# A hybrid decoder step with an expert lookup: tile border, sample path and depthwise convolution rearranged

## The reference, cut to what matters

```
x += W_out [ window attention | conv branch ] (rmsnorm(x) W_in)
x += peer(rmsnorm(x))
x += (p W_ple) * sigmoid(rmsnorm(x) W_gate)

conv branch: y[t, c] = sum over j < 31 of w[j, c] * glu[t - 30 + j, c] + bias[c]; layer norm; silu   (512 channels)
peer:        for each token 8 heads x 16 experts = 128 choices (top 16 of each of two key lists per head, then top 16 of their 256 sums)
             act = gelu(u[choice] . h); x += sum over the 128 choices of softmax weight * act * v[choice]
```

## Time and profile before

| | |
|---|---|
| time, median of 3 (range) | 3282.76 us (3281.87 to 3284.22) |
| profiled execution: its own time, its span | 3279.73 us, 3278.0 us |
| mean granted TensorE clock | 0.92 |
| busy share: TensorE, VectorE, ScalarE, GpSimd | 79%, 78%, 38%, 30% |
| mixer (until the first gather) | about 579 us |
| experts | about 2699 us |
| gathers | 1032, 1082 MB |

### The profile page before, as it was taken

One profiled execution on the slowest core, in us unless ns is written; L12 is line 12 of the kernel. 1 busy time (PEld: TensorE's weight loads), 2 busy tenths in 40 slices (PEclk: granted clock), 3 DMA queues, 4 the chain that ended last, 5 costly groups with the idle time before them and its releaser, 6 DMA issues.

```text
span 3278.0 us, 28593 instructions
## 1 busy us (share of the span) xinstructions
PE 2598.7 (79%) x8010; PEld 1279.4 (39%) x8010; DVE 2543.9 (78%) x5806; ACT 1252.6 (38%) x3574; POOL 999.5 (30%) x1072
## 2 busy tenths in 40 slices
PE   6899898777877788778777877787778777878778
PEld 3555444433433343334333433343334333434322
DVE  4889884898886888688868886888688868885555
ACT  2332323343443334433443344334433443344233
POOL 1000000343433333333333333333333333333241
PEclk8999998899999898999989988998989889989899
DMA  6000003999999999999999999999999999999996
GB/s 208 20 26 32 26 29 123 415 406 420 420 408 420 420 420 399 420 420 416 403 420 420 416 400 420 420 419 400 419 420 419 396 420 420 420 404 418 403 397 268
DMA packets 169961, 1144.79 MB, mean 349 GB/s; under 512 B 21376, under 2 KB 25072, under 8 KB 36688
## 3 DMA queue, kind: packets, MB, share of 16 engines
q0 software_dynamic: 148608, 1082.20, 80.2%
q1 hardware_dynamic: 21208, 60.94, 5.3%
HBM read 1133.85 MB, written 10.72 MB: 349 GB/s over the span
## 4 chain that ended last, share of the span: by engine, by line
DMA 34%; PE 21%; DVE 18%; issue 5%; ACT 5%; POOL 1%; ACTq 0%; POOLq 0%; DVEq 0%
DMA arena<-in_peer_uv_dram,arena 34%; PE VA L1573 15%; DVE arena L1373 7%; PE QB L1606 3%; PE QB L1553 2%; DVE XP L1384 2%; DVE arena L1304 2%; DVE arena L1301 2%; DVE arena L1308 1%; ACT arena L1175 1%; ACT L1165 1%; ACT arena L1168 1%; POOL arena L1109 1%; DMA arena<-arena 1%; ACT L1154 1%
## 5 line engine op out<-in xcount | busy, mean ns | idle before, releaser
L1573 PE MATMUL VA<-arena 128*128 128x512 f32 x3232 | 1663.6, 654 | 571.2 <-ACT arena L1175 494.0
L1373 DVE CUSTOM_DVE_ANT_0 arena<-arena,HP 128x1024 f32<-128x1024 f32 x1024 | 1232.3, 1218 | 517.0 <-DMA arena<-in_peer_uv_dram,arena 507.8
L1109 POOL DMA_INDIRECT arena<-in_peer_uv_dram,arena x1032 | 978.0, 948 | 1702.5 <-PE VA L1573 894.7
L1573 PEld LDWEIGHTS VA<-arena 128*128 128x128 f32 x3232 | 619.7, 205 | 1455.2 <-ACT arena L1175 796.3
L1165 ACT ACTIVATE arena<-arena 128x1 f32<-128x1 f32 x1024 | 206.2, 201 | 1369.4 <-DVE arena L1373 1354.3
L1175 ACT ACTIVATE arena<-ident,arena 128x128 f32<-128x128 f32 x808 | 324.4, 401 | 77.1 <-ACT arena L1168 3.0
L1168 ACT ACTIVATE arena<-arena 128x1 f32<-128x1 f32 x1024 | 301.5, 294 | 33.3
L1553 PEld LDWEIGHTS QB<-arena 128*128 128x128 f32 x2048 | 255.1, 197 | 64.6 <-issue 64.6
L635 DVE SCALAR_TENSOR_TENSOR arena<-arena 128x128 f32<-128x128 f32 x960 | 273.4, 347 | 7.9
L1384 DVE SCALAR_TENSOR_TENSOR XP<-arena,XP 128x1024 f32<-128x1024 f32 x208 | 267.1, 1284 | 0.1
L1553 PE MATMUL QB<-arena 128*128 128x128 f32 x2048 | 254.1, 279 | 2.6 <-PEq L202 2.6
(11 more groups left out here) (208 smaller groups left out, 1502.6 us busy)
## 6 DMA issues: line engine op xcount, KB each, us to landing
arena<-in_peer_uv_dram,arena POOLq DMA_INDIRECT x1032, 12.9
arena<-x SPq DMA_DIRECT2D x17, 512.0 KB, 7.8
arena<-in_x_prompt_dram SPq DMA_DIRECT2D x16, 512.0 KB
arena<-in_peer_wq_dram SPq DMA_DIRECT2D x8, 1024.0 KB, 14.5
arena<-in_w_in_dram SPq DMA_DIRECT2D x8, 896.0 KB, 12.7
x<-arena SPq DMA_DIRECT2D x8, 512.0 KB
arena<-in_w_ple_gate_dram SPq DMA_DIRECT2D x1, 4096.0 KB, 28.1
arena<-sample_h SPq DMA_DIRECT2D x8, 512.0 KB, 20.4
```

What stands on the lines that cost most here:

```text
L1109: nc.gpsimd.indirect_dma_start(rows[slot(turn)], None, peer_uv, bass.IndirectOffsetOnAxis(ap=index, axis=0)).then_inc(landed[slot(turn)], 16)
L1373: nc.vector.tensor_tensor_reduce(out=u_row(turn), in0=u_row(turn), in1=HP[:, :], scale=1.0, scalar=0.0, op0=ALU.mult, op1=ALU.add, accum_o ...
L1573: last = nc.tensor.matmul(VA[:, c:c + BANK], diag[:, n % DIAGS, :], v_row(turn)[:, c:c + BANK], start=v_turn(k) == 0, stop=v_turn(k) == PE ...
```

## The change

Five edits go in together.

1. *Border.* The last `add_row(127)` writes XP + its term straight into `xf`; `finish_x` is gone. x itself is added to XP in the middle of the tile: `add_x(t)` on VectorE at row 44. At j = 0, ahead of row 0's dot product, VectorE does `add_row(f, 127)` and `finish_x2`. ScalarE makes row 127's weight ahead of `place_h`.
2. *Parts.* `RANK_AT` becomes (42, 64, 86, 108) for all tiles; the last part's pairs, exp and names come 10 rows later than the others' (its pairs at j = 10 and 13 of the next tile instead of 2 and 5). rank_norm, turn_h, take_hT, gate_sigmoid, finish_sum move by 2 to 4 rows to fit.
3. *Sample's h.* The store to DRAM and the 8 loads go; at rows 75 to 82 TensorE multiplies a column of the identity, spread over 128 columns, with h's 8 rows (4 instructions a token), and ScalarE copies the result to `h_bc` (128x1024) one row later.
4. *Sample's rows.* `SAMPLE_AT` moves from 92 to 95, the final steps by 2 to 3 rows.
5. *Convolution.* For each chunk of 128 channels one tensor_tensor multiplies 128 overlapping windows of 31 tokens with the 31 taps (3968 products for a partition), one tensor_reduce adds each 31; one more instruction adds the bias. Chunk 0 stands where the first 7 taps stood, chunk 1 where the next 7, chunks 2 and 3 where the last 17.

```diff
-SAMPLE_AT = tuple(range(92, 92 + 2 * NB, 2))
+SAMPLE_AT = tuple(range(95, 95 + 2 * NB, 2))
+X_AT = 44
-RANK_AT = (38, 62, 86, 110)
-RANK_FIRST_AT = (42, 64, 87, 110)
+RANK_AT = (42, 64, 86, 108)
+LAST_PART_DELAY = dict(DELAY, pairs0=30, pairs1=33, exp=35, names0=36, names1=39)
...
-            def conv_tap(j):
-                for c in range(CT):
-                    src, w = gluT[:, c, j:j + P], chan[:, c, j:j + 1]
...
+            def conv_chunk(c, steps):
+                line = gluT[:, c, 0:P]
+                windows = bass.AP(tensor=line.tensor, offset=line.offset, ap=[list(line.ap[0]), [1, P], [1, TAPS]])
+                steps.link(TT(products, windows, chan[:, c, 0:TAPS].unsqueeze(1).to_broadcast([P, P, TAPS]), ALU.mult))
+                steps.link(nc.vector.tensor_reduce(acc[:, c, :], products, AX.X, ALU.add))
...
-                for j in range(FIRST_TAPS, FIRST_TAPS + EARLY_TAPS):
-                    steps.link(conv_tap(j))
+                conv_chunk(1, steps)
...
-                for j in range(FIRST_TAPS + EARLY_TAPS, TAPS - 1):
-                    steps.link(conv_tap(j))
-                conv_tap(TAPS - 1).then_inc(conv_done, 1)
+                conv_chunk(2, steps)
+                conv_chunk(3, steps)
+                TT(acc[:, :, :], acc[:, :, :], chan[:, :, TAPS].unsqueeze(2).to_broadcast([P, CT, P]), ALU.add).then_inc(conv_done, 1)
...
-            for n in range(NB):
-                sp.dma_start(h_bc[:, n, :], h_dram[n].partition_broadcast(P)).then_inc(hbc_landed, 16)
...
                     if t and j == 0:
-                        place_h(t)
                         row_weight(t - 1, CHOICES - 1)
+                        place_h(t)
...
+                        if 76 <= j < 76 + NB:
+                            act.wait_ge(h_spread, j - 75)
+                            nc.scalar.activation(h_bc[:, j - 76, :], QB[:, :], ACT.Copy).then_inc(hbc_ready, 1)
...
-                    nc.vector.scalar_tensor_tensor(out=XP[:, :], in0=v_row(turn), scalar=weight, in1=XP[:, :],
+                    nc.vector.scalar_tensor_tensor(out=xf if k == CHOICES - 1 else XP[:, :], in0=v_row(turn), scalar=weight, in1=XP[:, :],
...
+            def add_x(f):
+                dve.wait_ge(xf_landed, (f + 1) * 16)
+                dve.wait_ge(vd_used, f * DVE_ROWS + sum(by_vector(k) for k in range(X_AT - 2)))
+                steps.link(TT(XP[:, :], XP[:, :], xf, ALU.add))
...
-                        if j == 1:
+                        if j == 0:
                             add_row(f, CHOICES - 1)
-                            finish_x(f)
-                        if j == 2:
                             finish_x2(f)
...
+                        if 75 <= j < 75 + NB:
+                            n = j - 75
+                            if n == 0:
+                                pe.wait_ge(ssc_copied, 1)
+                            else:
+                                pe.wait_ge(hbc_ready, n)
+                            for c in range(0, D, BANK):
+                                last = nc.tensor.matmul(QB[:, c:c + BANK], ident[0:NB, n:n + 1].to_broadcast([NB, P]), hq[0:NB, c:c + BANK],
+                                                        start=True, stop=True)
+                            last.then_inc(h_spread, 1)
```

More of the change, by code:

```diff
@@ L83, in parts_at @@
     for p in range(len(STEADY)):
+        at = RANK_AT[p] + (LAST_PART_DELAY if p == len(STEADY) - 1 else DELAY)[stage]
         for q in (t, t + 1):
-            at = (RANK_FIRST_AT if q == 1 else RANK_AT)[p] + DELAY[stage]
             if 0 < q < NT and (q - 1) * CHOICES + at == t * CHOICES + j:
@@ L263, in mixer @@
         assert take.at[0] <= AHEAD, take.at[0]
+        products = arena[:, ARENA - P * TAPS:ARENA].rearrange("p (t j) -> p t j", j=TAPS)
         const_made, const_in, out_w_in = sem("const_made"), sem("const_in"), sem("w_out_in")
@@ L626, in residual, with first_chunk @@
                 TT(x_res[0:R, :], ZB[0:R, bank * BANK:(bank + 2) * BANK], x_res[0:R, :], ALU.add).then_inc(x1_ready, 1)
-            def conv_tap(j):
-                for c in range(CT):
-                    src, w = gluT[:, c, j:j + P], chan[:, c, j:j + 1]
-                    if j == 0:
-                        last = nc.vector.tensor_scalar(acc[:, c, :], src, w, chan[:, c, TAPS:TAPS + 1], ALU.mult, ALU.add)
-                    else:
-                        last = nc.vector.scalar_tensor_tensor(out=acc[:, c, :], in0=src, scalar=w, in1=acc[:, c, :],
-                                                              op0=ALU.mult, op1=ALU.add)
-                return last
-            def first_taps(t, steps):
+            def conv_chunk(c, steps):
[3 more added lines that the diff above has]
+                steps.link(nc.vector.tensor_reduce(acc[:, c, :], products, AX.X, ALU.add))
+            def first_chunk(t, steps):
                 dve.wait_ge(gluT_copied, t + 1)
-                for j in range(FIRST_TAPS):
-                    steps.link(conv_tap(j))
+                conv_chunk(0, steps)
             def prompt_tile(t, next_rows, norm_rows, first=False):
@@ L676, in prompt_tile @@
                     x_norm(t + 2, norm_rows, steps)
-                    first_taps(t + 1, steps)
-                assert steps.n == (D_STEPS if norm_rows else D_STEPS - 1 - FIRST_TAPS), steps.n
+                    first_chunk(t + 1, steps)
+                assert steps.n == (D_STEPS if norm_rows else D_STEPS - 1 - FIRST_STEPS), steps.n
             steps = Chain(dve, dve_step)
@@ L689, in _ @@
             x_norm(1, P, steps)
-            first_taps(0, steps)
+            first_chunk(0, steps)
             dve.wait_ge(const_made, 3)
@@ L700, in _ @@
             t, R, rows = NT, NB, HEADS * NB
-            steps = Chain(dve, dve_step, t * D_STEPS + D_FIRST - 1 - FIRST_TAPS)
+            steps = Chain(dve, dve_step, t * D_STEPS + D_FIRST - 1 - FIRST_STEPS)
             dve.wait_ge(s_ready, t + 1)
@@ L1244, in _ @@
                         x2_square(f, P)
-                    if t and j == 25:
+                    if t and j == 27:
                         gate_sigmoid(f, P)
-                    if j == 29:
+                    if j == 33:
                         rank_norm(q)
-                    if j == (40 if t == 0 else 36):
+                    if j == 40:
                         take_hT(q)
@@ L1383, in add_row, with finish_x2 @@
                     dve.wait_ge(vd_used, n)
-                    nc.vector.scalar_tensor_tensor(out=XP[:, :], in0=v_row(turn), scalar=weight, in1=XP[:, :],
+                    nc.vector.scalar_tensor_tensor(out=xf if k == CHOICES - 1 else XP[:, :], in0=v_row(turn), scalar=weight, in1=XP[:, :],
                                                    op0=ALU.mult, op1=ALU.add).then_inc(vd_used, 1)
-            def finish_x(f):
+            def add_x(f):
+                dve.wait_ge(xf_landed, (f + 1) * 16)
+                dve.wait_ge(vd_used, f * DVE_ROWS + sum(by_vector(k) for k in range(X_AT - 2)))
+                steps.link(TT(XP[:, :], XP[:, :], xf, ALU.add))
+            def finish_x2(f):
                 dve.wait_ge(vd_used, (f + 1) * DVE_ROWS)
-                dve.wait_ge(xf_landed, (f + 1) * 16)
-                steps.link(TT(xf, XP[:, :], xf, ALU.add))
-            def finish_x2(f):
                 dve.wait_ge(vp_used, (f + 1) * PE_ROWS)
@@ L1521, in _ @@
             add_row(LAST, CHOICES - 1)
-            finish_x(LAST)
             finish_x2(LAST)
@@ L1579, in turn_p @@
                 if f == SAMPLE:
-                    pe.wait_ge(ssc_copied, 1)
+                    pe.wait_ge(hbc_ready, NB)
                 elif f == LAST:
@@ L1637, in _ @@
                 for j in range(CHOICES):
-                    if j == (38 if t == 0 else 34):
+                    if j == 38:
                         turn_h(q)
@@ L1653, in _ @@
                     if t == LAST:
-                        if j == 28:
+                        if j == 33:
                             turn_p(LAST, P)
-                        if j == 31:
+                        if j == 35:
                             ple_product(LAST, P)
                         for chunk in range(CHUNKS):
-                            if j == 38 + 2 * chunk:
+                            if j == 40 + 2 * chunk:
                                 sample_queries(chunk)
```

58 lines of the change are left out of this document (27 added, 31 removed).

## The result

The changed kernel takes 3268.31 us (median of five runs, 3259.93 to 3270.53) against 3282.76, a ratio of 0.9953 [0.9942, 0.9963]: 14.5 us faster where 48 were forecast, and outside the forecast's range. The profiled run is the one of 3268.31; its span is 3266.6. Own time against own time the two profiled executions differ by 11.4 us (3279.73 and 3268.31); the other 3.0 are that the median before lay above its profiled execution.

What follows compares the result with a forecast made beforehand. An engine or ring of engines bounds the mixer, the DMA's gathers at 420 GB/s the experts stage. Gains 20 + 10 + 6 + 2 + 11, less 1, make 48 us: 3231.7, said as 3235 us, range 3224 to 3257.

Steps and rivals of the forecast that it cites:

- Border, 20 us: At seven tile borders, 25.3 us lost to DMA starving; an earlier first XP leaves 0.8 us each: 20 us gained.
- of each the loss is (420 - v) / 420 x 81.95 us: Prices each border slice's GB/s below 420 as lost time: 25.3 us for seven borders, 3.6 each.
- nothing back: Lower bound of the gain at the tile borders; the upper bound was all 25.3 us.
- the border does not come back: Rival: `x2_square` on ScalarE starves the DMA at borders, only some 5 of the 20 come; 3250 us, chance 0.15.
- x at row 44 and parts later, 0: Mid-tile: adding x is hidden by the DMA with margin 17 us; moved pairs are the same work: 0 us each.
- Sample's h and end, 10 + 6 + 2 in, 0 for the spread: Last tile: dropped transfers gain 10.0 us, shorter waits 6, the shorter end 2; the TensorE spread costs 0.
- It falls 4 us behind; the ring's 12.9 us hide that: Last tile's spread: TensorE needs 24 us where the DMA brings 8 rows in 20; the buffers hide it: 0.
- the spread runs at the low clock: Rival in the last tile: four matmuls take 3.78 us, not 1.98; 16 us lost, 3251 us, chance 0.08.
- The 2 us of the end: Behind the last gather: `finish_x` (1.22) leaves the chain and last buffers free earlier; 2 us gained, bounds 0 and 4.
- Convolution, 11 us: Mixer: the piece on the path falls from 28.1 to 26.7 us, 1.4 a tile; eight tiles gain 11, bounds 5 and 18.
- Overlapping windows: Rival in the convolution: overlapping windows are read slowly, the product takes twice its time; 3355 us, chance 0.07.
- The sum: Whole kernel: 20 + 10 + 6 + 2 + 11 = 49, less 1 for moved rows: 48 us gained.

Runs made afterwards that it cites:

- border_plan: Kernel before with the border's order, x at row 44 and the ranking's new rows, without spread and convolution: nothing gained in whole time; row 30 to row 30 2289.4 us.
- before_no_rank: Kernel before without VectorE's lists, pairs and names from tile 1 on, all tiles gathering tile 0's experts: no border dip; GpSimd waits 5.20 us there for 8.06.
- after_again: The changed kernel measured once more, nothing altered: runs at 3257.7 and 3259.2 us against 3269.8 to 3271.6; its profiled run 3269.9.
- conv_only: Kernel before with the convolution's edit alone: 4.1 us faster in whole time; first gather issued at 572.07, 7.4 us ahead of the kernel before.
- no_spread: Changed kernel with the sample's h spread by the eight transfers again instead of by TensorE, sample rows at 92, 94, ...: 3275.0 us.

## Why the prediction was wrong, point by point

*Border, 20 us: 5.2.* The dip went and the waits fell, though not each as worked out: the first XP came 2.5 us earlier for 4.3, GpSimd waited 5.51 us where about 4 was forecast, TensorE 5.16 where about 8 was. The step that failed is "of each the loss is (420 - v) / 420 x 81.95 us", read as a price that goes away with its place. By the runs the seven tiles gave 5.2 us in the changed kernel and in border_plan, of which 1.9 in the first tile, and the rest of the price came back as dips in the middle, which went only with the ranking (13.4 us in seven tiles, 2289.4 to 2276.0). The bound "nothing back" was on record and was the nearer end; the value was taken at the other. By what the ranking's time holds up the gathers is open.

*Its rival, "the border does not come back": right in outcome, wrong in cause.* `x2_square` stands in before_no_rank as before, and nothing dips.

*x at row 44 and parts later, 0: right as far as seen.* No engine waited for `add_x`, and it did not wait itself in any of its 8 times.

*Sample's h and end, 10 + 6 + 2 in, 0 for the spread: the largest miss.* Behind row 30 of the last tile the changed kernel lost 1.6 us where 18 were to be gained. The waits went as forecast; the cover failed. "It falls 4 us behind; the ring's 12.9 us hide that" reckoned at 1.98 us. TensorE waited for a copy (1.11 us), ran at a granted clock of 0.50 (1.2 GHz) and then needed 7.4 us for a token and a row where the DMA brings a row in 2.5. That is the rival "the spread runs at the low clock", priced at 16, given 0.08; 7 runs of 11 lie in the upper group that goes with it, and at the median the spread's matmuls cost 12. The 2 us of the end are 0.5 here; in after_again's profile the piece behind row 127's dot product took 26.1 us, here 28.5, before 29.0, so this term is not known to better than 2 us.

*Convolution, 11 us: 8.0 at the first gather.* The piece from `residual` to the last instruction went from 31.9 to 30.4 us in the tile shown, 1.5 a tile where 1.4 was forecast. But VectorE waited longer for TensorE at `residual`, 24.0 us over the mixer's tiles instead of 21.5: the other side of the ring did not come earlier by as much. Overlapping windows did not slow the product: 4286 ns for 3968 elements, the same as the reduce, which reads them in a row; 4.33 us was forecast.

*The sum:* 14.5 of 48. Between the two profiled executions it is 7.9 (convolution) + 5.2 (border) - 1.6 (last tile) = 11.4, and 3.0 more are the median of before above its profiled execution. The whole times of the parts built singly (4.1, 0 and 6.7) don't add up to this, since conv_only, border_plan and no_spread each wait longer at `sample_pairs` (11.99, 15.49 and 18.0 us) than the kernel before did.

## What to carry to other kernels

A dip in a saturated stream shows where a loss comes to light, not who causes it: before pricing its removal, leave the suspected work out of the whole period, or put a stall of its size back, and see whether the period's length moves. Compare periods between two marks that stand at the same place in both kernels, and look at the waits of the stretch behind them before a part's whole time is taken as its price. A step that is to be hidden beside such a stream has to be priced at TensorE's lower clock as well, if TensorE waits anywhere in it; here spacing it out gave 6 to 7 us at the median, the whole border 5.2.

## What was not expected of the hardware

- VectorE in stretches of 3 us, 60 us in a tile of 328, costs the gathers 1.4 to 1.9 us a tile, although one ring buffer less costs only 0.8 and VectorE waits for gathers 61.7 us in the same tile (waits of VectorE in tile 1 of the changed kernel: total, times, longest). How the one brings about the other is open.

```profile
DVE arena L1366 <- DMA arena<-in_peer_uv_dram,arena: 61.7, 56, 3.4
```

- In these dips the DMA's share stays at 1.00 and only the GB/s fall (391 to 397): the share alone shows no loss.
- The Trainium skill, *VectorE: DVE Perf Modes*, Rules for kernel authors, calls `tensor_reduce` the slowest VectorE operation. The trace doesn't bear that out: at 3968 elements it took 4286 ns, and so did the product. The Trainium skill gives (N + 151) / 0.96 ns for a float32 tensor_tensor (the same page, The TRN2 errata); for 3968 elements that is 4291 ns, an estimate from that page, and the product's 4286 agrees.
